# Latent attention computed four heads and 128 tokens at a time: heads packed into halves and quarters of the TensorE array, division applied to the weighted sums

## The reference, cut to what matters

```python
def mla_group(c_q, c_kv, k_pe_raw, pos_f, q_norm, w_uq, kv_norm, w_ukv):
    B, S, _ = c_q.shape; H = MLA_HEADS                                       # 512 tokens, 8 heads
    q = (rms_norm(c_q, q_norm) @ w_uq).reshape(B, S, H, 64 + 32)             # QK_NOPE_DIM + QK_ROPE_DIM
    q_nope, q_pe = q[..., :64], rope(q[..., 64:], pos_f)
    kv = (rms_norm(c_kv, kv_norm) @ w_ukv).reshape(B, S, H, 64 + 64)
    k_nope, v = kv[..., :64], kv[..., 64:]
    k_pe = rope(k_pe_raw[:, :, None, :], pos_f)[:, :, 0]                     # one 32-wide key part for all heads
    s = einsum('bqhd,bkhd->bhqk', q_nope, k_nope) + einsum('bqhr,bkr->bhqk', q_pe, k_pe)
    p = softmax(s * MLA_SCALE, axis=-1)                                      # over 512 keys, no mask
    return einsum('bhqk,bkhd->bqhd', p, v)
```

## Time and profile before

| | us |
|---|---|
| median of 3 runs | 2116.93 (2114.89 to 2124.73) |
| the profiled execution | 2118.26 |
| its span | 2116.1 |
| busy in it: PE, DVE, ACT, POOL | 2008.6, 1203.6, 966.0, 930.5 |
| first query matmul to first scores (33 us of projections) | 1582.9 to 1616.2 |
| first scores to first matmul of the output projection | 1616.2 to 1700.8 |

### The profile page before, as it was taken

The page is one execution under the profiler, slowest core; times in us unless marked ns, Lnnn a source line. Parts: engine busy times, 40 slices in busy tenths (PEclk is TensorE's granted clock), DMA queues, the critical chain, the costliest instruction groups (busy, mean ns, idle before and its releaser), DMA issues.

```text
span 2116.1 us, 35025 instructions
## 1 busy us (share of the span) xinstructions
PE 2008.6 (95%) x12650; PEld 1748.5 (83%) x12650; DVE 1203.6 (57%) x1723; ACT 966.0 (46%) x1629; POOL 930.5 (44%) x522
## 2 busy tenths in 40 slices
PE   7899999899998999999889999999989899999998
PEld 7899999897776799978679997886773377999787
DVE  5766651384365777760377776117557627777611
ACT  4566632324323465642346665325345424666522
POOL 3255454433325355554435555543333033555542
PEclk9999999899999999999999999999999999999999
DMA  5133333222211233333213333332211022333331
GB/s 154 55 105 99 97 110 93 60 63 80 70 53 58 70 109 103 105 107 93 70 50 110 109 103 106 96 100 80 65 40 30 1 70 60 110 106 102 109 95 54
DMA packets 333739, 177.40 MB, mean 84 GB/s; under 512 B 9404, under 2 KB 329143, under 8 KB 333647
## 3 DMA queue, kind: packets, MB, share of 16 engines
q1 hardware_dynamic: 331792, 175.07, 28.4%
q10 hardware_dynamic: 1854, 1.06, 0.2%
HBM read 174.01 MB, written 2.10 MB: 83 GB/s over the span
## 4 chain that ended last, share of the span: by engine, by line
PE 79%; DVE 10%; issue 5%; ACT 3%; POOL 2%; DMA 0%; SPq 0%; ACTq 0%; POOLq 0%; DVEq 0%
PE ps L2009 40%; PE ps L2155 32%; POOL wlo L402 2%; DVE wa L1460 1%; PE ps L2640 1%; DVE E L1485 1%; DVE xop_f L1235 1%; PE ps L2037 1%; PE ps L2606 1%; DVE xlo L1182 1%; DMA raw<-in_ffn_w_in 0%; DVE small L1889 0%; ACT xop L574 0%; DVE xop L1259 0%; PE ps L2349 0%
## 5 line engine op out<-in xcount | busy, mean ns | idle before, releaser
L402 POOL TENSOR_TENSOR wlo<-raw,whi 128x1024 fp32r<-128x1024 f32 x192 | 485.1, 2536 | 658.1 <-ACT whi L526 657.3
L2155 PE MATMUL ps<-xop,whi 128*128 128x256 f32 (+1 forms) x4032 | 724.0, 282 | 11.6 <-DVE wlo L1301 5.9
L2155 PEld LDWEIGHTS ps<-xop,whi 128*128 128x128 f32 x4032 | 622.5, 189 | 13.5 <-DVE wlo L1301 6.4
L2155 PE MATMUL ps<-xop,wlo 128*128 128x256 f32 (+1 forms) x2016 | 568.8, 282 | 0.0
L459 POOL TENSOR_TENSOR wlo<-raw,whi 128x512 fp32r<-128x512 f32 x212 | 288.1, 1363 | 223.8 <-ACT whi L599 223.8
L2155 PEld LDWEIGHTS ps<-xop,wlo 128*128 128x128 f32 x2016 | 380.2, 189 | 0.0
L2009 PE MATMUL ps<-xop,whi 128*128 128x512 f32 (+1 forms) x1120 | 326.5, 352 | 13.3 <-POOL wlo L402 8.2
L526 ACT ACTIVATE whi<-raw 128x1024 fp32r<-128x1024 f32 x176 | 183.6, 1052 | 277.1 <-PE ps L2009 268.8
L2009 PE MATMUL ps<-xhi,whi 128*128 128x512 f32 (+3 forms) x720 | 248.0, 376 | 38.3 <-DVE xlo L1182 18.1
L2009 PE MATMUL ps<-xop,wlo 128*128 128x512 f32 (+1 forms) x880 | 280.9, 352 | 0.0
L2009 PE MATMUL ps<-xlo,whi 128*128 128x512 f32 (+3 forms) x720 | 239.6, 364 | 0.0
(11 more groups left out here) (343 smaller groups left out, 2727.1 us busy)
## 6 DMA issues: line engine op xcount, KB each, us to landing
raw<-in_ffn_w_in SPq DMA_DIRECT2D x88, 512.0 KB, 3.7
raw<-in_ffn_w_gate SPq DMA_DIRECT2D x44, 512.0 KB, 3.8
raw<-in_ffn_w_up SPq DMA_DIRECT2D x44, 512.0 KB, 3.7
raw<-in_ffn_w_out SPq DMA_DIRECT2D x32, 512.0 KB, 3.5
raw<-in_ffn_w_down SPq DMA_DIRECT2D x32, 512.0 KB, 3.5
raw<-in_a_w_in SPq DMA_DIRECT2D x24, 512.0 KB, 3.7
raw<-in_w_in SPq DMA_DIRECT2D x19, 512.0 KB, 3.8
raw<-in_ffn_w_out SPq DMA_DIRECT2D x16, 384.0 KB, 3.0
```

What stands on the lines that cost most here:

```text
L402: pool.tensor_tensor(wlo[:, u % SLOTS, :], raw[:, u % SLOTS, :], whi[:, u % SLOTS, :].bitcast(F32), ALU.subtract).then_inc(lo_done, 1)
L2155: ins = pe.matmul(ps[:, bank_, 0:h], w[l][:, k * P:(k + 1) * P], x[r][:, k * h:(k + 1) * h], start=start and k == 0 and q == 0, stop=k == ...
```

## The change

- **Layout.** The 96 query rows of a head are no longer together. `units2` loads the weights with columns regrouped ("q0", "q1", "kv", "k_pe", four, four, two and four DMAs in place of one each), so that one 128-row tile holds the rope parts of four heads (`qp`, 32 rows each), and one the plain parts of two (`qn`, 64 rows each). Keys `kn` hold two heads a tile. `kpe` holds four copies of the shared key part (its weight columns are loaded four times). MLA_SCALE is put into the copy of the queries.
- **Projections.** Six query tiles of six matmuls, two rope products of 128 rows instead of eight of 32, four key tiles of three matmuls, the values as before. POOL's part in the rope (`pool_rope`) is gone, DVE does all three steps; ACT and DVE share the copies.
- **Attention.** The unit of work u = 0..7 is four heads (g = u // 4) by 128 queries (c = u % 4). Its scores fill four banks: four matmuls with 64 rows in the two halves of the array, then four with 32 rows in the four quarters, added to the same banks. Four maxima (negated by the instruction), four exponentials. Four tiles are turned through two banks, copied once by ACT and three times by DVE. The weighted sums are 16 matmuls of 128 columns in two halves of the columns.
- **Division.** The probabilities are not scaled. For each group of four units DVE takes `v.reciprocal` of the 16 sums of a query, each repeated 64 times (two instructions with 128 x 512 outputs), PE transposes these (`spread_recips`), ACT copies them to `rbs`, and DVE multiplies the 128 x 512 weighted sums by them.
- **Output projection.** `pe_out` is gone; its first two tiles are made in parts (`out_part`) inside `pe_mla`, four input tiles before the last attention steps and four behind, in banks 0 and 1.

```diff
-        for h in range(HEADS):
-            for c in range(CH):
-                turn(h, c)
-                nh, nc_ = (h + 1, c + 1) if c + 1 < CH else (h + 2, 0)
-                if nh < HEADS:
-                    dots(nh, nc_)
...
+        for u in range(1, 2 * CH + 1):
+            if u < 2 * CH:
+                dots(u)
+            else:
+                pe.wait_ge(s["P_exp"], QUAD * (u - 1) + 2)
+                pe.wait_ge(out_s["v_ready"], out_at[4]["v_ready"] + 2)
+                out_part((4, 5))
+            if u == CH + 1:
+                spread_recips(0)
+                weighted(u - 2, 0)
+                weighted(u - 2, 1)
+            for j in range(QUAD):
+                turn(u - 1, j)
+                if j in (1, 2) and u >= 2 and u != CH + 1:
+                    weighted(u - 2, j - 1)
+        out_part((6, 7))
+        spread_recips(1)
+        weighted(2 * CH - 1, 0)
+        weighted(2 * CH - 1, 1)
+        out_part((0, 1, 2, 3))
...
+        def dots(u):
+            g, c = u // CH, u % CH
+            span = slice(c * P, (c + 1) * P)
+            for pair in range(2):
+                if u >= 1:
+                    pe.wait_ge(s["P_exp"], QUAD * (u - 1) + 2 * pair + 2)
+                for i in range(2):
+                    rows = slice(NOPE * i, NOPE * (i + 1))
+                    pe.matmul(ps[:, 2 * pair + i, :], m3["qn"][rows, 2 * g + pair, span], m3["kn"][rows, 2 * g + pair, :],
+                              start=True, stop=False, skip_group_check=True)
+            for j in range(QUAD):
+                rows = slice(ROPE_DIM * j, ROPE_DIM * (j + 1))
+                pe.matmul(ps[:, j, :], m3["qp"][rows, g, span], m3["kpe"][rows, :], start=False, stop=True,
+                          skip_group_check=True).then_inc(s["dots"], 1)
...
+        def recips(g):
+            v.wait_ge(s["P_exp"], CH * QUAD * (g + 1))
...
+                v.reciprocal(tile(wa, pair, SEQ).rearrange("p (c j n) -> p c j n", c=CH, j=2),
+                             total.broadcast_to([P, CH, 2, V_DIM])).then_inc(s["recip"], 1)
...
+            for k in range(CH):
+                for i in range(2):
+                    j = 2 * pair + i
+                    h = QUAD * g + j
+                    ins = pe.matmul(ps[V_DIM * i:V_DIM * (i + 1), 6 + pair, c * P:(c + 1) * P],
+                                    m3["vm"][:, k, h * V_DIM:(h + 1) * V_DIM], pt_tile(u, j)[:, k * P:(k + 1) * P],
+                                    start=k == 0, stop=k == CH - 1, skip_group_check=True)
```

More of the change, by code:

```diff
@@ L98, in constants @@
     swap("perm", range(P), RET_DIM // 2)
[L99 removed]
+    swap("permpe", range(P), ROPE_DIM // 2)
     for b in range(P // RET_DIM):
@@ new lines, in out_hi @@
+        def out_hi(m):
+            act.wait_ge(s["o_scaled"], m + 1)
+            act.activation(tile(xhi, m, SEQ), tile(wb, m % 2, SEQ), ACT.Copy).then_inc(s["o_hi"], 1)
+        split_to(act, u0)
+        for q in (0, 1, 2):
+            keep_query(q)
+        act_deviation(act, 3)
+        split_to(act, u0 + 1)
+        for q in (4, 5):
+            keep_query(q)
+        keep_key(0)
+        keep_key(2)
+        keep_value(0)
+        for u in range(CH * 2):
+            if u == 5:
+                keep_recips(0)
+            if u >= 1:
+                keep_turned(u - 1)
+            for j in range(QUAD):
+                scores_exp(u, j)
+                if u == 0 and j == 1:
+                    keep_value(2)
+            if u == 0:
+                act_ret_hi(act, 3)
+            if u in (1, 2):
+                split_to(act, u0 + 1 + u)
+            if u == 6:
+                out_hi(0)
+                out_hi(1)
@@ new lines, in dve_mla @@
+        rope(0)
+        keep_query()
+        rope(1)
+        keep_key(1)
+        keep_key(3)
+        keep_value(1)
+        for j in range(QUAD):
+            maximum(0, j)
+        keep_value(3)
+        dve_normed(v, 3)
+        for u in range(1, 2 * CH):
+            maximum(u, 0)
+            maximum(u, 1)
+            keep_turned(u - 1, 1)
+            maximum(u, 2)
+            maximum(u, 3)
+            keep_turned(u - 1, 2)
+            keep_turned(u - 1, 3)
+            if u == 1:
@@ new lines, in spread_recips, with out_part @@
+        def spread_recips(g):
+            pe.wait_ge(s["recip"], 2 * (g + 1))
+            last = CH * (g + 1) - 1
+            for pair in range(2):
+                pe.wait_ge(s["PT_dve"], 3 * last + 2 + pair)
+                for c in range(CH):
+                    ins = pe.transpose(ps[:, 4 + pair, c * P:(c + 1) * P], tile(wa, pair, SEQ)[:, c * P:(c + 1) * P], ident[:, :])
+                ins.then_inc(s["rb_turned"], 1)
+        def out_part(tiles):
+            for k in tiles:
+                pe.wait_ge(*((a2["r_split"], k - 3) if k >= 4 else (s["o_split"], k + 1)))
+                for m in range(2):
+                    if k == 4:
+                        pe.wait_ge(lo_done, u0 + 3 + m + 1)
+                    ins = product(pe, [ps[:, m, :]], w_tile(u0 + 3 + m, k), [x_cols(k, META, SEQ)], k == 4, k == 3)
+                    if k == 3:
+                        ins.then_inc(unit_done, 1)
```

460 lines of the change are left out of this document (231 added, 229 removed).

## The result

| | before | after |
|---|---|---|
| median, us | 2116.97 (2114.89 to 2124.73) | 2090.34 (2088.94 to 2098.14) |
| the profiled execution, its span | 2118.26, 2116.1 | 2091.44, 2089.4 |
| first query matmul to first scores | 33.3 | 15.4 |
| first scores to the end of the weighted sums | 84.7 | 78.6, of which 5.6 are output projection |
| the rest, with those 5.6 | 415.3 | 420.3 |

The ratio is 0.9875, with a 95% interval from 0.984 to 0.991: 26.6 us, or 1.25%, faster. The forecast was 2092, from 2080 to 2105.

A forecast was written before the change was run, and what follows sets the result against it. PE's count of passes bounds the kernel, weakly also the score-to-exponential chain. Savings of 16.8 (projections) and 11.5 (attention), less 0.2 (rope) and 3.5 (clock), took 2118.3 to 2093.7, so median 2092 us, range 2080 to 2105.

The forecast's parts named there:

- Projections: First query pass to first scores: 54 passes at 0.244 us plus swaps and variance, 16.5 us instead of 33.3, 16.8 saved.
- the 0.2 for DVE's rope: In the projections: charge for DVE's rope of the second group not hidden beside POOL's work, 0.2 us, ends 0 and 3.
- Packing: In attention's products: pairs fully concurrent, and a group of four 512-column products all at once, 0.86 us.
- The second and third rival: Attention: array quarters not all concurrent, 2099 or 2106 us, chance 0.13; 512-column packs serial, 2126 us, chance 0.08.
- The unit: One steady attention unit: PE the bound at 7.0 us (scores 3.0, transpositions 1.9, weighted sums 2.05), against 10.3.
- The reciprocals: DVE's 512-element reciprocals: 3.7 us each from a slope of 7.0 ns an element, with PE and ACT standing behind unit 5's scores.
- The first rival: Attention's large reciprocals are quick, 0.69 us; waits and clock falls go, 2081 us, chance 0.17.
- The waits: PE idle behind the first and the last pair of reciprocals: 5.1 and 2.6 us.
- Attention as a whole: First scores to the end of the weighted sums: 73.2 us without output projection, against 84.7; 11.5 saved.
- 3.5 for the clock: PE clock falls behind the reciprocal waits: 2.5 us after the first pair, 1.0 after the last, 0 to 7 together.
- The two units about the spread: From the end of unit 4's scores, behind the first reciprocals: 21.7 us for two units instead of 14.0.
- The fourth rival: PE in attention: clock falls for good under packed or short products; 49 us more in all eight units, 2141, chance 0.05.

## Why the prediction was right, and where it was off

The forecast was 1.7 us above the median, and on its own basis 2.3 (2093.7 against the profiled 2091.4). That is closer than its terms were; they were off on both sides.

- **Projections**: 16.5 forecast, 15.45 measured, 17.8 saved instead of 16.8. The count was right. The passes cost 0.233 each where the earlier trace rows had given 0.244 over the first twelve (0.6 in all), swaps and variance 0.95 instead of 1.03, and the 0.2 for DVE's rope were not needed: its slow step beside POOL came, 2.8 us where the earlier trace rows had 2.17, and was hidden.
- **Packing**: right in kind. The group of quarters takes 1.07 where 0.86 and a change of form were charged, the halves and columns as forecast. The second and third rival, which hung on it, are out.
- **The unit**: 7.24 against 7.0. Scores 2.99 (3.0), sums 2.05 (2.05); the turns 2.2 instead of 1.9, because three of them each carry a change of form that I had charged to the scores alone. PE was the bound, as said; exponentials stood 0.67 apart, not the 0.86 I had charged, and no steady unit waited for them.
- **The reciprocals**: mechanism, place and the engines that stand were right, and so was taking the slope. 3.32 us against 3.7: the slope from one to eight elements (7.0 ns) was a little too steep. The Trainium skill, "VectorE: DVE Perf Modes", "First, the fixed hardware budget", with its repeat count of 8, gave an estimate of 4.3; the trace shows a cost for each element, and a smaller one. The first rival, quick reciprocals at 2081, is out as a description, but a kernel that really has them runs at 2079 to 2085.
- **The waits**: 4.34 and 1.64 us, forecast 5.1 and 2.6; off by 0.8 and 1.0. Two reciprocals stand ahead of each, and account for 0.8 (2 x 3.7 against 6.6).
- **Attention as a whole**: 73.0 measured, with the clock's 2.2 in it. Forecast were 73.2 and, apart, 3.5 for the clock. The fall behind the first pair came (2.2 us; 2.5 charged), the one behind the last did not (1.0 charged). The other 2.4 us lie in three places. To the end of unit 4's scores 31.0 were forecast and 30.0 measured, although the steady units took 7.2 and not 7.0: the sum had charged four full units there, but PE has no turns and no weighted sums to make between the first and the second scores, and no weighted sums before the third; waits (1.3 and 0.6) took back only a part. The two units about the spread took 23.0, or 20.8 without the clock, against 21.7; the last unit 7.2 against 7.0; the tail 12.8 against 13.5. In the two units and in the tail the reciprocals are worth up to 0.8 each; the exponentials and the longer turns share the rest, which I haven't taken apart.
- **Not in the sum**: the profile of after came 2.2 us earlier to the first query pass, where PE's work is the same up to there, and lost 5.0 behind attention to the clock. These, 2.8 net, ate most of the 5 us by which projections and attention beat the forecast. The 2.2 are mostly the clock too: from 640 to 730 us it was granted at 0.92 before and 0.94 after, 1.8 us. The base was lucky as well. Attention and projections took 118.0 us in the profile from which the forecast subtracts, but 120.8 and 121.0 in the two later ones of before, each with two half-clock stretches there. A range of 25 us covered all that; a point that agrees to 2 us did so partly by luck.
- **The fourth rival** (clock down for good) did not come. The kernel with serial quarters shows something near its mechanism: with 32-row products one after another the clock fell while PE was busy, for 3.4 or 6.8 us at a time and not for good. The packed products, of which the rival spoke, kept 1.00.

## What to carry to other kernels

Price an instruction by its own rows even far outside their range: the slope between one and eight elements told the cost of 512 to an eighth (3.7 against 3.32), where the cost of "any other 512-element instruction" would have been out by a factor of five. Take the reciprocal before you repeat the value, not of the repeated value. Packing products with few rows is worth most of its factor (3.4 of 4 in quarters, 1.9 of 2 in halves), but count each change of form (0.1 to 0.15 us). Before moving work off an engine, look whether that engine was the bound: here DVE had room for the division where it was. Before comparing two executions by their totals, compare their granted clock ahead of the stage that was changed.

## What the runs showed of the hardware

- Float32 products of 32 rows and 512 columns in four quarters of the array take 1.07 us for four, against 3.63 one after another; halves 1.92 for four against 3.62.
- A DVE reciprocal costs about 6 ns for each element written, repeated inputs or not (3319 ns for 512), a copy that repeats values 0.42 us for the same output.
- The clock fell to its lower level within units in which PE had 13.20 us of work in 13.41, in the kernel with serial quarters (0.75 granted). It stayed full with the same products packed.
- The same wait of 2.0 us in the same program (the second late wait of the changed kernel) was followed by a half-clock stretch in one execution (0.82 granted over 9.5 us) and not in the other (1.00 over 12 us). The same program reached the same instruction 7.4 us apart in two profiles, with 0.97 and 0.95 granted over 190 us of the way and 0.98 and 0.95 over 137 us.
